# State space branch of a two-layer kernel: identity products as transposes, and a group's squares added on GpSimd before one sum over partitions

## The reference, cut to what matters

```
y_off  = einsum('bclgn,bcgrpn,bcgrl->bclgrp', Cc, h_prev, exp(a_cs))
y      = (y_diag + y_off)  in both directions, + d_skip * xs
u      = y * silu(z)                       # then by group of 512 channels
u      = u * rsqrt(mean(u * u, axis=-1) + eps) * g
```

## Time and profile before

| | |
|---|---|
| median of three runs | 2254.39 us |
| the three runs | 2250.88, 2254.74, 2254.39 us |
| span of the profiled execution | 2250.8 us |
| PE busy over the span | 82% |
| DVE, ACT, POOL busy | 41%, 33%, 8% |

### The profile page before, as it was taken

How to read it: one execution, slowest core, us unless ns; L and a number is a source line. 1 busy time by engine, 2 the same in 40 slices (tenths; PEclk the granted TensorE clock), 3 DMA queues, 4 the chain that set the end, 5 groups by cost and what they waited for, 6 DMA issues and landing times.

```text
span 2250.8 us, 26956 instructions
## 1 busy us (share of the span) xinstructions
PE 1847.5 (82%) x10850; PEld 1171.9 (52%) x10850; DVE 913.3 (41%) x1608; ACT 750.6 (33%) x1294; POOL 179.3 (8%) x183
## 2 busy tenths in 40 slices
PE   6999999999987656556565565656999999989999
PEld 4766777889952111111111111112956888768887
DVE  5363877885550000000000000002657747787745
ACT  4343567676321000000000000003455535675533
POOL 0210022253011000000000000000000000320000
PEclk8999999999998787877888878787999999999999
DMA  9534243355599999999999999998524554324562
GB/s 365 210 134 168 95 123 110 104 170 203 216 410 428 428 428 429 428 429 429 428 429 429 428 429 428 428 428 343 183 80 171 187 225 162 137 83 177 188 237 97
DMA packets 68166, 619.07 MB, mean 275 GB/s; under 512 B 8272, under 2 KB 17232, under 8 KB 22624
## 3 DMA queue, kind: packets, MB, share of 16 engines
q1 hardware_dynamic: 56464, 598.98, 65.5%
q10 hardware_dynamic: 9248, 10.49, 1.8%
q0 software_dynamic: 2352, 8.19, 1.1%
HBM read 616.52 MB, written 1.11 MB: 274 GB/s over the span
## 4 chain that ended last, share of the span: by engine, by line
PE 54%; DMA 37%; DVE 5%; ACT 2%; issue 1%; POOL 0%; SPq 0%; DVEq 0%; ACTq 0%; POOLq 0%
DMA ring<-in_w_edown 18%; DMA ring<-in_w_eup 17%; PE bank L535 10%; PE bank L537 10%; PE bank L536 10%; PE bank L2919 5%; PE bank L2921 3%; PE bank L2711 3%; PE bank L2728 2%; PE bank L3362 1%; PE bank L1870 1%; PE bank L1294 1%; DMA ring<-in_w_ada 1%; PE bank L1202 1%; DMA ring<-in_w_in_qk 1%
## 5 line engine op out<-in xcount | busy, mean ns | idle before, releaser
L506 DVE TENSOR_TENSOR ring_parts<-ring,ring_parts 128x2048 fp32r<-128x2048 f32 (+2 forms) x125 | 280.8, 2251 | 164.9 <-ACT ring_parts L500 164.6
L2815 DVE TENSOR_TENSOR work<-bank,work 128x512 f32<-128x512 f32 x14 | 9.7, 692 | 804.3 <-PE bank L2711 804.3
L500 ACT CAST ring_parts<-ring 128x2048 fp32r<-128x2048 f32 (+3 forms) x151 | 276.5, 1834 | 174.5 <-DMA ring<-in_w_mlp_out 80.8
L2711 PE MATMUL bank<-ring,work 128*32 128x512 f32 x1024 | 170.7, 801 | 134.7 <-DMA ring<-in_w_egate 69.5
L2728 PE MATMUL bank<-ring,work 128*32 128x512 f32 x1020 | 174.2, 817 | 98.8 <-DMA ring<-in_w_edown 92.0
L2711 PE MATMUL bank<-work 128*32 128x512 f32 x1024 | 153.2, 728 | 87.5 <-DMA work<-in_w_eup 61.5
L535 PE MATMUL bank<-hT_hi,ring_parts 128*128 128x256 f32 (+2 forms) x584 | 195.8, 335 | 1.1 <-POOL ring_parts L517 0.8
L537 PE MATMUL bank<-hT_hi,ring_parts 128*128 128x256 f32 (+2 forms) x584 | 186.7, 320 | 0.0
L536 PE MATMUL bank<-hT_lo,ring_parts 128*128 128x256 f32 (+2 forms) x584 | 186.5, 319 | 0.0
L2919 PE MATMUL bank<-hn_parts,ring_parts 128*128 128x512 f32 x512 | 179.9, 396 | 0.0
L2711 PEld LDWEIGHTS bank<-ring,work 128*32 128x32 f32 x1024 | 33.8, 128 | 263.1 <-issue 109.7
(11 more groups left out here) (472 smaller groups left out, 3513.1 us busy)
## 6 DMA issues: line engine op xcount, KB each, us to landing
ring<-in_w_edown SPq DMA_DIRECT2D x62, 2048.0 KB, 26.2
work<-in_w_eup SPq DMA_DIRECT2D x33, 2048.0 KB, 27.3
ring<-in_w_egate SPq DMA_DIRECT2D x33, 2048.0 KB, 26.0
work<-in_w_egate SPq DMA_DIRECT2D x31, 2048.0 KB, 25.8
ring<-in_w_eup SPq DMA_DIRECT2D x31, 2048.0 KB, 26.3
ring<-in_w_mlp_in SPq DMA_DIRECT2D x32, 1024.0 KB, 4.8
ring<-in_w_mlp_out SPq DMA_DIRECT2D x30, 1024.0 KB, 4.9
ring<-in_w_ada SPq DMA_DIRECT2D x12, 2048.0 KB, 9.2
```

What stands on the lines that cost most here:

```text
L500: act.copy(halves_of(name, ring_parts)[1], halves_of(name, ring)[0]).then_inc(hi_made, 1)
L506: dve.tensor_tensor(lo, halves_of(name, ring)[0], hi, ALU.subtract).then_inc(lo_made, 1)
L2711: last = pe.matmul(bank[which][32 * n:32 * n + 32, :], rows[:, 2 * c + k2, :], w[:, k2, 512 * n:512 * n + 512], start=c == 0 and k2 == 0, ...
```

## The change

Three things change. The two identity products of each `pair_product` get the transpose flag. The four products with ones of a group become one, on `ysq[:, 0]`, and that stands behind `turn(g, 4)` (in the last group behind `gates(12)`). POOL adds the squares of blocks 1, 2 and 3 into slot 0, at places between its chunk splits.

```diff
             for t in range(TT):
                 pe.matmul(o[:, t * P:(t + 1) * P], yoff[:, t, blk * P:(blk + 1) * P], ident, start=t == 0, stop=False,
-                          skip_group_check=True)
+                          is_transpose=True, skip_group_check=True)
...
-        def squares_sum(pe, g, blocks):
+        def squares_sum(pe, g):
+
+            pe.wait_ge(y_added, GB * (g + 1))
+            pe.matmul(squares_bank(g)[:, 0:L], ones, ysq[:, 0, :], start=True, stop=True).then_inc(y_tot, 1)
+
+        def add_squares(pool, g, blocks):
 
             for blk in blocks:
-                pe.wait_ge(y_sq, GB * g + blk + 1)
-                pe.matmul(squares_bank(g)[:, 0:L], ones, ysq[:, blk % 2, :], start=blk == 0, stop=blk == GB - 1).then_inc(y_tot, 1)
+                pool.wait_ge(y_sq, GB * g + blk + 1)
+                if blk > 1:
+                    pool.wait_ge(y_added, GB * g + blk)
+                pool.tensor_tensor(ysq[:, 0, :], ysq[:, 0, :], ysq[:, 1, :], ALU.add).then_inc(y_added, 1 if blk > 1 else 2)
...
         def ssd_pool(pool):
 
+            squares_after = {"gates_6": (SSD_G - 1, (1, 2, 3))}
+            for g in range(SSD_G - 1):
+                squares_after[f"c{g + 1}"] = (g, (1,))
+                squares_after[f"xs{g + 2}_0" if g + 2 < SSD_G else "gates_0"] = (g, (2, 3))
...
                 split_lower_pool(pool, name)
+                if name in squares_after:
+                    add_squares(pool, *squares_after[name])
...
                 gate_block(g, 2)
-                if g:
-                    pe.wait_ge(y_gated, GB * g - 1)
-                    squares_sum(pe, g - 1, (0, 1))
                 turn(g, 2)
                 gate_block(g, 3)
                 turn(g, 3)
+                turn(g, 4)
                 if g:
-                    squares_sum(pe, g - 1, (2, 3))
-                turn(g, 4)
+                    squares_sum(pe, g - 1)
                 scores(g)
...
             gates(10)
-            squares_sum(pe, g, (0, 1))
             gates(11)
-            squares_sum(pe, g, (2, 3))
-            for i in range(12, GATES):
+            gates(12)
+            squares_sum(pe, g)
+            for i in range(13, GATES):
                 gates(i)
...
                     act.wait_ge(y_gated, nb + 1)
-                    if nb >= 2:
-                        act.wait_ge(y_tot, nb - 1)
-                    act.activation(ysq[:, blk % 2, :], yT[:, nb, :], ACT.Square).then_inc(y_sq, 1)
+                    if blk < 2:
+                        act.wait_ge(y_tot, g)
+                    else:
+                        act.wait_ge(y_added, nb)
+                    act.activation(ysq[:, min(blk, 1), :], yT[:, nb, :], ACT.Square).then_inc(y_sq, 1)
```

More of the change, by code:

```diff
@@ L1688, in build @@
              "y_tot", "y_std", "y_norm"))
+        y_added = sem("y_added")
         abc_in = [sem(f"abc_in{i}") for i in range(2)]
@@ L2052, in squares @@
                     act.wait_ge(y_gated, nb + 1)
-                    if nb >= 2:
-                        act.wait_ge(y_tot, nb - 1)
-                    act.activation(ysq[:, blk % 2, :], yT[:, nb, :], ACT.Square).then_inc(y_sq, 1)
+                    if blk < 2:
[3 more added lines that the diff above has]
+                    act.activation(ysq[:, min(blk, 1), :], yT[:, nb, :], ACT.Square).then_inc(y_sq, 1)
             def root(g):
-                act.wait_ge(y_tot, GB * g + GB)
+                act.wait_ge(y_tot, g + 1)
                 if g:
```

## The result

| | before | after |
|---|---|---|
| median | 2254.56 us (4 runs) | 2270.09 us (4 runs) |
| range of the runs | 2250.88 to 2256.61 | 2266.51 to 2272.97 |
| profiled span | 2250.8 us | 2264.7 us |

What follows compares the result with a forecast made beforehand. PE was taken as the bound. Wait 4.3, `normalise` 0.85, last group -1.2, tail 0 and clock 1.6 gave +5.5 us: 2259.9 us, say 2260, from 2254.4; range 2251 to 2267.

Steps and rivals of the forecast that it cites:

- the wait, less the savings, with root and tail: State space stage: 4.3 us of later iterations, 0.85 at the root, less 1.2 in the last group, tail 0; +3.9 us.
- The wait ahead of the one product: Iterations 1 to 3: PE waits 3.95 us for POOL's last add, making each iteration 1.43 us later, 4.3 in all.
- The rival that the adds come in time: After turn 4: last add ends by 467.8 us, PE never waits, 2244 to 2246 us; chance 0.12 with a half-way case.
- I lay out iteration 3 in the times of before, as DVE holds them: Iteration 3: DVE's timeline, with no idle entry in the 36 us up to 461.94, was taken to keep its old times.
- Coming earlier with PE's products brings DVE nothing: Iteration 3: DVE's gapless work was claimed to gain nothing from earlier PE products.
- The clock: Behind PE's three waits in the stage: one fall to half clock counted, 1.6 us, bounds 0 and 4.8.
- The third rival: Clock falls in every wait, +8.7 us, or `normalise` wholly under POOL in iteration 3, to +11.2: 2263 to 2266; chance 0.10.
- `normalise` under POOL: Iteration 3: one of DVE's four products falls under POOL's second chunk, 0.85 us more at `carried`, bounds 0 and 3.4.
- The transposes: Identity products of each of 16 blocks: 0.31 us less a block, 5.0 us of PE work.
- the bound 0: Lower bound of the saving per block: the transpose flag buys nothing in an open bank; upper bound 0.42 us.
- the tail: Last group, from `gates(10)` to the output projection: 16.0 us against 16.1, saves nothing; bounds 1.4 saved, 2 lost.
- The shift reaches the end: Behind the stage: everything hangs on it through PE and the ring slots it frees, so the +5.5 us carries through.

Runs made afterwards that it cites:

- e11: Full change plus eight dead products filling PE's wait ahead of the one product, and SP's 1 MB load held until six of eight decays; ratio 1.0020 to before.
- e6: Full change plus SP's 1 MB ring load held back until ACT has made six of the previous group's eight decays; ratio 1.0045 to before.
- e4: Full change plus eight dead products filling PE's wait ahead of the one product in each of the first three groups; ratio 1.0040 to before.
- e8: The full change once more, unaltered, run beside other kernels on the same chip; ratio 1.0091 to before.
- e2: Full change without the transpose flag: only the adds on POOL and one product a group; ratio 1.0048 to before.
- e10: Full change with all three of POOL's adds ahead of the four pieces of the next chunk; ratio 1.0052 to before.
- e3: Full change with a group's one product moved behind the next iteration's first projection (iteration 3: first gate block); ratio 1.0041 to before.
- e7: Full change with the one product moved an iteration on, and SP's 1 MB load held until six of eight decays are made; ratio 1.0021 to before.
- e5: Kernel before plus the transpose flag alone, and SP's 1 MB load held until six of eight decays are made; ratio 0.9989 to before.
- e14: Kernel before with ACT's second decay-sums transfer waiting for the projection that releases SP's load, no transposes or adds; ratio 0.9999 to before.
- e13: Kernel before plus transposes and SP's load held back, with POOL's adds and the one product for the last group alone; ratio 0.9985 to before.

## Why the prediction failed, step by step

Between before and after lie 11.77 us in the stage. e11 is the change with clock and sums kept in order by filler and hold: +3.66. The other 8.11 us can be split at the start of the one product. Up to it, counted from `carried`, late sums can delay an iteration and the clock cannot, since what a fall slows stands behind the product; from it to the next `carried` it is the other way round:

| us | `carried` to the product | product to the next `carried` |
|---|---|---|
| e11 filler, hold | 47.04 47.04 47.04 | 15.76 15.73 12.00 |
| e6 hold | 46.97 46.98 46.99 | 15.79 17.44 12.14 |
| e4 filler | 49.33 48.81 47.95 | 15.80 15.78 12.02 |
| after | 48.19 48.51 47.97 | 17.30 18.48 12.25 |
| e8 full, again | 48.63 48.44 48.25 | 18.69 17.43 12.80 |

The two columns part cleanly: with the hold the first stays at 47.0, with the filler the second stays at 15.8 and 12.0. After is 3.55 us over e11 in the first and 4.54 in the second.

| term | forecast | measured |
|---|---|---|
| the wait, less the savings, with root and tail | 4.3 + 0.85 - 1.2 + 0 = 3.9 | 3.66 |
| decay sums late | none | 3.55 (4.2 in e8) |
| clock | 1.6 | 4.54 (5.4 in e8) |
| behind the stage | 0 | about 3.5 in this execution |

The single executions differ, after and e8 by 1.5 us in the stage though they are one kernel, so the terms are good to a microsecond or so.

1. **The wait ahead of the one product** was right in cause and size: 3.95 us forecast, 3.58 measured, 1.43 us an iteration forecast, 1.36 and 1.33 in e11. The product was forecast 47.2 us behind `carried` (471.75 less 424.55) and stands at 47.0 in e6 and e11, where the wait in e6 is 3.22. It is released by POOL's last add, behind four pieces. The rival that the adds come in time is out.
2. **"I lay out iteration 3 in the times of before, as DVE holds them" is the step that failed.** "Coming earlier with PE's products brings DVE nothing" was true as far as it went; I did not ask whether it could bring it a loss. I checked that the block products have room behind the masks (1.26 us for 1.24 of saving; in after PE has no wait there), and took the masks' own inputs as fixed. They were not: PE's earlier `b{g}` released SP's load sooner, the sums landed later, and ACT's first square, at 37.4 us behind `carried` in before's iteration 3 and 37.3 in e11, came at 38.3 to 38.8 in after, and POOL's chunk with it; the wait ahead of turn 2 is this lateness as PE sees it. A saving on PE moved a transfer that no instruction of the change touches. It cost 3.55 us of the stage in after, 4.2 in e8 and 5.0 in e4.
3. **The clock** is the second step that failed, by its count. One fall is worth 1.6 us by the forecast and 1.71 lacking by the windows (the windows of the earlier trace rows from 909 to 913 us lack 1.71 as well), so the size was right; but I counted one in three, and after had three, one of them twice as long. What they cost in time is less than they lack (4.5 of 6.8): 1.5 and 2.75 in iterations 1 and 2, 0.25 in the third, where the wait at `carried` covers most of it, which is 1.31 us in e11 and nothing in after. Of 17 waits of 2.4 to 3.6 us on PE in the stage (ahead of the product in after, e8, e2 and e6, at L535 in e10, at `carried` in e3 and e7) 15 saw a fall; e6's first (3.22 us) did not, nor did e3's (3.24 us). The Trainium skill (TensorE: Matmul & The Clock Gate, The HAM clock gate) says that full clock is taken back when PE idles; the traces agree for 15 of 17. I had weighed it down by the one idle of the earlier trace rows that kept its clock. The third rival (a fall in every wait, +8.7) was nearer than the forecast; with 3.55 for the late sums it comes to 12.3, against 11.8 measured in the stage.
4. **`normalise` under POOL, 0.85 us at `carried`.** In after it did not come: the four products took 1.67 us behind POOL's pieces, the wait of 0.70 was gone, since everything ahead was later. The chain is there all the same: in e11, with the other losses away, the first of the four took 1.10 us under POOL's last piece where it took 0.49 alone, and the wait is 1.31 instead of 0.70.
5. **The transposes.** 0.23 us a block, forecast 0.31, and the bound 0 is out. From the last `carried` to the merge they gave 0.96 us, together with the tail (forecast 1.2 and 0); e5, which has the flag alone, gives 0.74 of it there.
6. **"The shift reaches the end"** held. Behind the stage 3.5 us came on top. 1.33 of them are a wait for the rest of the last `w_out` chunk, whose load ACT awaited 5.80 us where the chunk before it took 3.90; of the other 2.1 the longer clock fall can account for 1.7 (5.12 lacking against 3.41). Timelines of ACT and PE after:

```profile
622.77 1.91 ACT L500 CAST ring_parts<-ring 128x2048 fp32r<-128x2048 f32 x1 [5.80 <-DMA ring<-in_w_out]
...
627.06 0.50 PE L535 MATMUL bank<-ring_parts,oT_hi 128*128 128x512 f32 x1 [1.33 <-DVE ring_parts L506]
```

In the nine executions with adds for every group that section took 81.3 to 83.9 us, but e14 has 82.0 without any.

**Open.** One chunk of `w_out` is awaited 5.4 to 6.6 us instead of some 4 in after, e3, e4, e7 and e11, and PE waits for it in the first, second and fourth of these (1.33, 2.10 and 1.57 us), but in no kernel without the last group's adds, nor in e8, e6 or e13. Why, and what decides how early the clock falls before the logits, no experiment isolates. By the medians the full change took +15.5 us in one set of runs and +17.9 in the other (ratios 1.0069 and 1.0091), and of that the stage explains 11.8 and 13.3.

## What to carry to other kernels

Taking work off the bounding engine also moves every transfer that its progress releases. List them, and ask of each which smaller transfer it now runs beside and who waits for that one; here the hold of one load an iteration by under 3 us gave back 3.3 us with the transposes alone and 6.4 in the full change, some 2.7 of these through fewer falls of the clock. A reduction shared between engines is priced by what is queued ahead of it on the slower engine: 0.75 us of add cost 3.6 us of wait behind four pieces, and moved ahead of them it made those late instead. And a wait of 2.4 us or more on a densely busy PE is to be counted with a fall of the clock each time (15 of 17 here), 1.5 to 1.7 us or, in the two longer falls, 2.7 to 2.9, unless a wait behind it covers it or something keeps PE busy, as the filler did.

## What the runs showed of the hardware

- A transfer of 256 KB on ACT's queue was ready for its reader 8.2 us after its issue where a 1 MB load on SP's queue followed it by 0.13 us, and 7.0 us where that followed by 0.34. The Trainium skill (DMA: Bandwidth & Descriptors, Issuing engines are not separate DMA queues) says that transfers run on the same 16 engines and interleave, whoever issues them; the trace agrees. How much 0.2 us of issue are worth was the surprise: 1.1 us of landing. All 48 such transfers of the sixteen traces fall in line: 4.4 to 5.1 us from issue to landing with the load 2.9 us or more behind (21 of them), 6.8 to 7.3 with it 0.33 or 0.34 behind (6), 7.3 to 9.0 with it within 0.15 on either side (21).
- Behind waits of 2.4 to 3.6 us the clock's falls lack 1.70 to 1.71 us in 13 of 15 cases, and twice as much (3.40 and 3.41) in the other two.
- Two fp32 128x128 products with the identity took 0.54 us (4 records) and two with the transpose flag 0.31 us (2 records), in an open bank.
